# Which queue loads an expert's second matrix: SyncE's or ScalarE's

## What is computed

```
hu  = xblk @ w_up_gate[e] + b_up_gate[e]      # 1024 x 2048 per expert
g, u = halves of hu, clipped
act = g * sigmoid(1.702 * g) * (u + 1)
y   = act @ w_down[e] + b_down[e]             # 1024 x 1024 per expert
out[token] = sum over its 4 experts of gate * y
```

## Time and profile before

| | us |
|---|---|
| median of three runs | 1778.68 |
| the profiled execution | 1778.97 |
| its span, first to last instruction | 1777.2 |
| TensorE busy in the span | 1741.8 |
| VectorE busy | 1421.3 |
| ScalarE busy | 1142.5 |
| GpSimd busy | 311.1 |

### The profile page before, as it was taken

How to read it: one execution, slowest core, us unless ns; L and a number is a source line. 1 busy time by engine, 2 the same in 40 slices (tenths; PEclk the granted TensorE clock), 3 DMA queues, 4 the chain that set the end, 5 groups by cost and what they waited for, 6 DMA issues and landing times.

```text
span 1777.2 us, 26531 instructions
## 1 busy us (share of the span) xinstructions
PE 1741.8 (98%) x8973; PEld 1286.7 (72%) x8973; DVE 1421.3 (80%) x1450; ACT 1142.5 (64%) x1122; POOL 311.1 (18%) x241
## 2 busy tenths in 40 slices
PE   6999999999999999999999999999999999999997
PEld 5777777777888867777777777777777777777765
DVE  4565676576656888988988898889888988898898
ACT  4544554464454567777777777777777777777783
POOL 0012102210210101212111211121112111211153
PEclk9999999999999999999999999999999999999999
DMA  7431333233127479999999999999999999999985
GB/s 209 131 96 48 106 95 94 58 108 94 48 96 258 165 237 396 402 382 374 354 376 372 382 351 375 374 378 355 373 378 373 355 376 377 366 363 372 377 337 235
DMA packets 159058, 488.44 MB, mean 275 GB/s; under 512 B 13186, under 2 KB 83122, under 8 KB 125520
## 3 DMA queue, kind: packets, MB, share of 16 engines
q1 hardware_dynamic: 151936, 471.48, 72.5%
q0 software_dynamic: 7088, 16.52, 2.7%
HBM read 479.43 MB, written 24.39 MB: 283 GB/s over the span
## 4 chain that ended last, share of the span: by engine, by line
PE 96%; DVE 2%; issue 1%; ACT 0%; DMA 0%; SPq 0%; DVEq 0%; ACTq 0%
PE psum L327 28%; PE psum L329 27%; PE psum L328 27%; PE psum L980 1%; PE psum L698 1%; PE psum L728 1%; PE psum L1016 1%; PE psum L964 1%; PE psum L714 1%; PE psum L664 1%; PE psum L681 1%; DVE wL L1713 1%; PE psum L762 0%; DMA xt<-in_x 0%; PE psum L895 0%
## 5 line engine op out<-in xcount | busy, mean ns | idle before, releaser
L1713 DVE TENSOR_TENSOR wL<-wraw,wH 128x2048 fp32r<-128x2048 f32 x388 | 882.6, 2288 | 125.8 <-ACT wH L425 123.2
L425 ACT ACTIVATE wH<-wraw 128x2048 fp32r<-128x2048 f32 x388 | 744.1, 1919 | 296.6 <-PE psum L329 281.6
L327 PE MATMUL psum<-wH,xTH 128*96 128x512 f32 x1040 | 418.3, 402 | 2.2 <-DVE wL L1713 2.2
L329 PE MATMUL psum<-wH,xTL 128*96 128x512 f32 x1040 | 409.8, 394 | 0.0
L328 PE MATMUL psum<-wL,xTH 128*96 128x512 f32 x1040 | 409.7, 394 | 0.0
L327 PEld LDWEIGHTS psum<-wH,xTH 128*96 128x96 f32 x1040 | 168.8, 162 | 74.4 <-DVE wL L1713 2.7
L329 PEld LDWEIGHTS psum<-wH,xTL 128*96 128x96 f32 x1040 | 168.6, 162 | 73.0 <-issue 0.9
L328 PEld LDWEIGHTS psum<-wL,xTH 128*96 128x96 f32 x1040 | 168.9, 162 | 69.9 <-issue 0.2
L327 PE MATMUL psum<-wH,aTH 128*96 128x512 f32 x496 | 196.4, 396 | 0.0
L329 PE MATMUL psum<-wH,aTL 128*96 128x512 f32 x496 | 194.9, 393 | 0.0
L328 PE MATMUL psum<-wL,aTH 128*96 128x512 f32 x496 | 194.4, 392 | 0.0
(11 more groups left out here) (272 smaller groups left out, 2167.5 us busy)
## 6 DMA issues: line engine op xcount, KB each, us to landing
wraw<-in_w_up_gate SPq DMA_DIRECT2D x256, 1024.0 KB, 6.8
wraw<-in_w_down SPq DMA_DIRECT2D x128, 1024.0 KB, 7.5
fraw<-in_w_in SPq DMA_DIRECT2D x68, 512.0 KB, 4.0
yd<-in_consts SPq DMA_DIRECT2D x8, 1024.0 KB, 8.0
wraw<-yd SPq DMA_DIRECT2D x3, 2048.0 KB, 11.0
wraw<-in_w_out SPq DMA_DIRECT2D x4, 1024.0 KB, 6.6
xt<-in_x SPq DMA_DIRECT2D x4, 512.0 KB, 6.4
hres<-in_x SPq DMA_DIRECT2D x4, 512.0 KB, 5.4
```

The lines of the kernel that those rows point to most:

```text
L327: nc.tensor.matmul(ps, lh, rh, start=start, stop=False)
L329: return nc.tensor.matmul(ps, ll, rh, start=False, stop=stop)
L425: nc.scalar.activation(wH[:, b % SPLIT, :], raw(b), ACT.Copy).then_inc(p_hi, 1)
L1713: V.tensor_tensor(wL[:, b % SPLIT, :], raw(b), wH[:, b % SPLIT, :].bitcast(F32), ALU.subtract).then_inc(p_lo, 1)
```

## The change

SyncE's `load_body` no longer issues the four down pieces. ScalarE's `body` issues them itself, from a new function `load_down`, at four places: behind `high` of pieces 3, 4, 5 and 6. Each keeps the wait, the destination, the source and the landing semaphore that it had on SyncE. The down pieces of expert 31, which SyncE loads behind its loop, stay there. Buffers, sizes and the number of transfers are the same.

```
             def load_body(e, begun=0):
                 for p in range(begun, 8):
                     load_piece(e, p, up_src(e, p))
-                for q in range(4):
-                    load_piece(e, 8 + q, down_src(e - 1, q))
...
+            def load_down(i, q):
+
+                wait_split(act, i, 2 + q)
+                act.dma_start(raw(8 + q).rearrange("p (k n) -> p k n", k=2),
+                              w_down[0][bass.ds(i - 1, 1), q * 2 * P:(q + 1) * 2 * P, :].rearrange("o (k p) n -> p (o k) n", p=P)).then_inc(wraw_in[(8 + q) % RAW], 16)
+
             def body(i, prefetch, place):
                 high(act, i, 3)
+                load_down(i, 0)
                 if place > 1:
                     y_evac(i - 2)
                 high(act, i, 4)
+                load_down(i, 1)
                 high(act, i, 5)
+                load_down(i, 2)
                 a_high(i - 1, None if place == 1 else used((i, 0), 0))
                 for b in range(6, 12):
                     high(act, i, b)
+                    if b == 6:
+                        load_down(i, 3)
                     if not prefetch and b < 10:
                         late_bias_high(b - 6)
```

## The result

| | before | after |
|---|---|---|
| median, us | 1778.82 (4 runs) | 1789.65 (1787.48 to 1790.96, 4 runs) |
| profiled execution, us | 1778.97 | 1787.48 |
| its span, us | 1777.2 | 1785.7 |

The ratio is 1.0059, 95% interval 1.0047 to 1.0071. The forecast was 1778.7 with a range to 1783.5, so it was wrong: I had forecast no change and had given a loss of over 0.2% a chance of 0.15.

What follows compares the result with a forecast made beforehand. The prediction took TensorE to set the pace in the steady loop, with slack behind it. Its four terms, 0 + 0 + 0 + 0 on the profiled 1778.97 us, 0.3 above the median, gave 1778.7 us, range 1776 to 1783.5.

Steps and rivals of the forecast that it cites:

- Terms one and two: Expert loop: SyncE gains nothing for its up loads, 0; ScalarE's four issues, 1.77 us per expert, hide in idle time, 0.
- Term three: Expert 1, at the routing: ScalarE's wait for piece 3 delays `high` 5 to 7; cost 0, at worst 0.4 us.
- Term four: Behind the routing: SyncE's small stores go out earlier, so the slow-transfer hole starts 7 us earlier; cost 0.
- The first rival: Expert 1's second down piece caught in the hole: stall 2.3 us, perhaps as much again; 1781 to 1783.5 us; chance 0.09.
- Two queues move fewer bytes: Expert loop: mixing two queues drops the rate below the needed 370 GB/s; at 350, 1839 us; chance 0.04.
- What would show it wrong: TensorE below full in the loop, `high` waiting for landings after 740, ScalarE issues above 2 us, TensorE waiting 655 to 700.

Runs made afterwards that it cites:

- e12: Changed kernel, but SyncE issues the down pieces of experts 1 to 5 in the old order, ScalarE those of 6 to 31: 1778.93 us, ratio 0.9995.
- e11: Kernel before, all loads on SyncE, but ScalarE executes the four waits for VectorE with no transfer behind them: 1779.19 us, ratio 0.9997.
- e2: Kernel before, all loads on SyncE, but the small stores and loads go out early, behind expert 1's first down piece: 1778.76 us, ratio 0.9997.
- e1: Changed kernel, but SyncE waits for VectorE's piece 5 of expert 1 before the small stores and loads, their old time: 1782.53 us, ratio 1.0026.
- e4: Changed kernel, but SyncE again issues the four down pieces of expert 1, before the small transfers: 1783.16 us, ratio 1.0027.
- e8: Changed kernel, but both small stores go out between experts 9 and 10, bias loads stay behind the routing: 1782.83 us, ratio 1.0035.
- e9: Changed kernel, but `gate_of` alone moved between experts 9 and 10; `over_list` and bias loads stay behind the routing: 1786.54 us, ratio 1.0037.
- e10: Changed kernel, but `over_list` alone moved between experts 9 and 10; `gate_of` and bias loads stay behind the routing: 1784.15 us, ratio 1.0026.

## Why the prediction was wrong

- **Terms one and two (SyncE relieved, ScalarE's issues): right.** e12 and the full stretches from 742 us on show both at 0. An issue took 0.38 us. ScalarE's time line in the steady loop, changed kernel:

```profile
1001.49 1.92 ACT L425 ACTIVATE wH<-wraw 128x2048 fp32r<-128x2048 f32 x1 [0.84 <-PE psum L329]
1003.52 0.38 ACTq L1418 DMA_DIRECT2D wraw<-in_w_down  x1
1004.09 1.03 ACT L1375 ACTIVATE ysb<-psum 96x1024 f32<-96x1024 f32 x1 [0.69 <-DVE wL L1722]
1005.12 1.92 ACT L425 ACTIVATE wH<-wraw 128x2048 fp32r<-128x2048 f32 x1
1005.89 0.38 ACTq L1418 DMA_DIRECT2D wraw<-in_w_down  x1
1007.90 1.92 ACT L425 ACTIVATE wH<-wraw 128x2048 fp32r<-128x2048 f32 x1 [0.86 <-PE psum L329]
```

  `y_evac` moved by about 0.8 us, 0.2 more than reckoned, and just fits; `high` 4 follows `high` 3 by 3.63 us as before. The second issue runs beside `high` 4 and costs ScalarE nothing, which I had only bounded.
- **Term three (ScalarE held at expert 1): right.** `high` 5 moved from 641.09 to 645.47, VectorE waited 0.26 us for it, and TensorE for neither; e11 shows the term at 0.
- **Term four failed.** It said: "An earlier hole gives more slack there, which is worth nothing." This is the step that failed: a term put at 0 that cost 8.9 us on TensorE between 650 and 683 us, 5.85 of waiting and 3.0 of lowered clock. I looked at where today's hole nearly reached TensorE (expert 2's piece 1) and not at the pieces in flight when the hole comes early, and I ordered them as one queue would. The early hole alone is indeed free: e2. It is not free with the second queue, since the pieces that it holds up then share with up pieces that are needed after them.
- **The first rival had the place and missed the size.** It priced one piece at the worst landing of one queue, 16.9 us: 2.3 us of stall, 1783.5 at most. Measured were 13.3 us for that piece, which TensorE did not wait for, and 24.1 for the last one, two below it in the same queue, with 5.85 us of stall in all and 3.0 for the clock. What the prediction held against the rival, "that stretch has idle transfer time today", was wrong too: with the store there, the DMA share is 0.74 and 0.82 at 21 and 38 GB/s. I had the sharing rule in hand, wrote beside the rival that it would "shorten the worst landing of the former and lengthen that of the latter", and so had its sign reversed for this backlog: a down piece that is behind nothing in its own queue still gets only every second packet, and its packets are half as long. By equal packet counts the down pieces get a third of 415 GB/s, 138, which is an estimate of 7.6 us per piece of 1 MB. The last three landed 7.2 and 8.4 us apart. In one queue at 415 GB/s it is 2.5. That sum could have been made from the rows and the lengths of the two pieces' rows, 8 and 4 KB.
- **Two queues move fewer bytes: no.** 370 GB/s in 900 to 1255 as in the earlier trace rows, and 421 in the backlog at 660 to 666.
- **What would show it wrong** had named TensorE waiting for VectorE between 655 and 700. It is there.

Open: why 512 bytes in rows of 4 take the DMA rate to some 30 GB/s for 10 us was not tried further. Open are also the wide spread of e1, e4, e8, e9 and e10, and the 2 us between the profiled run of the changed kernel (1787.5) and its median.

## What to carry to other kernels

In one queue the transfers of this kernel landed in the order of issue, and that order can be the order of need. Two queues gave up this order exactly where transfers had a backlog, and there the queue with the smaller packets got the smaller share. Before splitting loads over queues, look not at the steady state but at the stretch with the longest landings, and sum what each queue would get there.

## What the runs showed of the hardware

- A store of 128 rows of 4 bytes to HBM holds up the core's loads for some 8 us: 32 and 182 GB/s in 642 to 648 and 648 to 654 us with it (e9, DMA share 1.07 and 0.67), 125 and 411 without (e10). A store of 512 rows of 16 bytes alone did not (e10 early, e9 late).
- Two queues with work got equal packet counts (194 and 198; 144 and 145), not equal bytes.
- A transpose on TensorE that picks every second column of its input, 96 x 128: 278 ns against 246, its weight load 211 against 141.
- An issue on ScalarE (0.38 us at 1005.89) runs beside an activation already started there (1005.12 to 1007.04).
